# A fused two-layer forward pass on one Trainium2 core: the opening loads its norm weights with the transposed input, squares that input instead of `x`, and splits the third weight chunk in quarters

## The chip, the cores and the metric

The kernel runs on one core of a Trainium2 chip, as one program on five engines: TensorE (PE, with its weight loads shown as PEld), VectorE (DVE), ScalarE (ACT), GpSimd (POOL) and SyncE (SP), which here only starts DMA transfers. The metric is the device time of one execution in microseconds (us), lower is better. Everything is float32.

## The reference, cut to what matters

256 tokens of width 2048 pass through two layers. The part that the change touches is the first normalization and the first projection:

```python
def rms_norm(x, w):
    y = xf * lax.rsqrt(jnp.mean(xf * xf, axis=-1, keepdims=True) + EPS)
    return (y * w.astype(jnp.float32)).astype(x.dtype)
...
h = rms_norm(x, norm_mix_pre[l])
proj = jnp.einsum('bsd,dc->bsc', h, w_in[l])          # 2048 x 10240
qa, ka, va, qn, kn, vn, gates = jnp.split(proj, split_at, axis=-1)
qa = apply_rope(...); ka = apply_rope(...)            # first 2048 columns
...
x = x + rms_norm(y, norm_mix_post[l])                 # x itself is first needed here
```

After it come differential and neighbourhood attention, two gated projections, an output projection, a feed-forward part of width 8192, and a second layer with its own mixers. All of that is left as it is.

## The kernel before, in words

The work is a fixed sequence of 342 weight **chunks**. A chunk is four slices of 128 rows of a weight matrix, mostly 512 columns wide, so 1 MB. For each chunk, SP loads it into one of three `RAW` buffers. ACT copies it to `HI` (rounded to float32r, `high`, L506). DVE writes the remainder `LO = RAW - HI` (`low`, L922). PE then multiplies: for each 128-row slice and each of two token halves `t`, three products are accumulated in `acc`: input high by weight high, input high by weight low, input low by weight high. That makes 24 matmuls of 128x512 to a chunk. The input is split likewise in `ATH` and `ATL`.

The opening differs. `XT` holds the input transposed (16 slices of 128 features by 256 tokens). `x_high(k)` (ACT, L531) multiplies slice k by its norm weight and rounds it, `x_low(k)` (DVE, L926) makes the remainder. The factor 1/rms of a token is not applied there: it is a scale per row (`R0`) when a finished block of 512 columns is read out of `acc` (`evac`). It comes from the sum of squares of `x` (two ACT squares over `XS`, step `x sq`), a mean on DVE, and a power on POOL (`root`, named `r0`). Chunks 0 and 1 are loaded and split in quarters of 128x512 (`first`, L847 on ACT and L932 on DVE). Chunks alternate between column blocks 0 and 1: chunks 0, 2, 4, 6 make block 0, and 1, 3, 5, 7 block 1; chunks 2g and 2g+1 need slices 4g to 4g+3 of the input. `ahead` says that the splits of chunk n+2 stand at chunk n. A block of kind `rope` is read out on DVE: two multiplications by cosine and sine (L912) and two sums (L904) per token half. Then PE transposes the result, four 128x128 pieces each (`to_heads`, L1425).

The order on each engine is the order of the code, with semaphore waits in between. Before its first real work PE runs 20 small products on the constant tile `rst` (`warm`). SP's list of loads at the start is written out by hand in `sync`: whatever stands in it waits for all issues ahead of it. ACT starts the norm weights (`col`, all the per-feature vectors together, 69 KB) and the first four slices of `XT` from its own queue.

Of the kernel before, what the change touches and what calls it, by code (L numbers as in the profile page):

```python
# [7 lines left out]
F32 = mybir.dt.float32  # L8
# [21 lines left out]
C_PRE, C_MLP, C_N2, C_PE, C_CW, C_CB, C_LB, C_SUB, C_NW, C_IN = 0, 16, 32, 48, 64, 96, 104, 120, 122, 138  # L30
# [39 lines left out]
def program(nc, x, xt, w_in, w_a, w_b, w_out, w_up, w_down, w_in2, w_out2, w_pg, w_pe, p2,  # L70
            cols, lamv, rpb, rows, bif, cos_c, sin_c, nam_c, id_c, lvl_c, caus_c, out):
    with ExitStack() as ctx:
# [23 lines left out]
        ST = sb("st", [P, 96])  # L96
        MHALF = sb("mhalf", [P, 16])
# [82 lines left out]
        XT = m(32, 4096).rearrange("p (k s) -> p k s", k=16)  # L180
# [101 lines left out]
        for n, j, t in ((7, 0, 0), (7, 0, 1), (8, 1, 0), (9, 1, 1)):  # L282
# [54 lines left out]
        for g in range(1, 4):  # L337
            behind[2 * g - 2] = [("x", g, 0)]
# [12 lines left out]
        xt_ = xt.rearrange("p (k s) -> p k s", k=16)  # L351
# [3 lines left out]
        def sync(e):  # L355
# [11 lines left out]
            for n in range(2):  # L367
                for j in range(4):
                    load(RAW[n][:, 512 * j:512 * j + 512], w_in[j * P:(j + 1) * P, 512 * n:512 * n + 512], "first", n, j)
# [8 lines left out]
            raw(6)  # L378
            load(IDN[:, :], id_c[0], "id")
            load(LAMV, lamv.partition_broadcast(P), "lam")  # L380
            raw(7)
            load(NAM, nam_c, "nam")
            load(LVL[:, :, :, :], lvl_c, "lvl")
            load(CAU[:, :], caus_c, "cau")
            load(BIF[:, :], bif, "bif")
            for n in order[8:]:
                if n == 25:
# [32 lines left out]
        def gpsimd(e):  # L420
# [12 lines left out]
            e.memset(MHALF[:, :], -0.5).then_inc(s_pool.on("mhalf"))  # L433
            po.wait_ge(s_pool, LAST)
            e.memset(RST[:, :], 1.0).then_inc(s_pool.on("rst 1"))
            po.wait_ge(s_pool, LAST)
            e.memset(RST[:, 0:S:64], 0.0).then_inc(s_pool.on("rst"))
            for n in range(N_ALL):
                if n == 4:
# [49 lines left out]
        def scalar(e):  # L489
# [39 lines left out]
            def x_high(k):  # L529
                ac.wait_ge(loaded("col"), "col")  # L530
                e.activation(ATH[:, k, :], XT[:, k, :], ACT.Copy, scale=COL[:, C_PRE + k:C_PRE + k + 1]).then_inc(  # L531
# [19 lines left out]
            def da(u):  # L551
                if 0 <= u - 3:
                    v = u - 3
                    h, t = divmod(v, 2)
                    ac.wait_ge(s_pe, "da back", v)
# [1302 lines left out]
```

## Time and profile before

| | |
|---|---|
| median of 3 runs | 1990.64 us (1989.63 to 1991.04) |
| the profiled execution | 1989.69 us, of which its span is 1987.9 us |
| PE busy | 1968.0 us (99%), 9456 matmuls |
| DVE, ACT busy | 1210.1 us (61%), 987.4 us (50%) |
| DMA | 369.25 MB, mean 186 GB/s |

The time of a run has 1.8 us outside the span in the profiled execution. PE is the engine whose busy share fills the span. The profile's busy time of PE takes matmuls that overlap their neighbours at their whole duration, so the start times of successive matmuls tell more than the busy share. The granted TensorE clock is 0.998 of full over the span.

### The profile page before, as it was taken

How to read it: one execution, taken by the hardware profiler on the slowest of the kernel's cores; microseconds unless marked ns; L12 is line 12 of the kernel's file. 1: busy time of each engine (PE TensorE's matmuls, PEld its weight loads, DVE VectorE, ACT ScalarE, POOL GpSimd, SP SyncE). 2: the span in 40 equal slices, each digit the busy share in tenths (PEclk: the TensorE clock that was granted, in tenths of full speed). 3: DMA queues.
4: the chain of work that ended last, by engine and by line, in shares of the span. 5: the costliest groups of instructions: out<-in, count | busy, mean ns of one | idle time of the engine just before them, and what ended most of it. 6: DMA issues, size and time to landing. Idle time of an engine off the chain costs nothing.

```text
span 1987.9 us, 22811 instructions
## 1 busy us (share of the span) xinstructions
PE 1968.0 (99%) x9456; PEld 1651.6 (83%) x9456; DVE 1210.1 (61%) x1142; ACT 987.4 (50%) x953; POOL 39.8 (2%) x42
## 2 busy tenths in 40 slices
PE   9999999999999999999999999999999999999998
PEld 7888888888888888888888888888889888878886
DVE  5746446644656655445566666677567869676564
ACT  6345544445445444444455555565455545444454
POOL 0000000000000000000000000000000000230000
PEclk9999999999999999999999999999999999999999
DMA  8663555555657356655555555565556454445462
GB/s 319 207 201 129 170 191 183 178 178 190 221 181 254 119 178 189 192 184 182 185 190 192 192 196 197 197 214 189 170 154 203 164 172 158 153 165 206 169 212 106
DMA packets 186009, 369.25 MB, mean 186 GB/s; under 512 B 6829, under 2 KB 14257, under 8 KB 185265
## 3 DMA queue, kind: packets, MB, share of 16 engines
q1 hardware_dynamic: 184888, 366.27, 55.5%
q8 instruction: 74, 1.21, 0.2%
q10 hardware_dynamic: 1016, 1.52, 0.2%
q14 instruction: 31, 0.25, 0.0%
HBM read 365.66 MB, written 2.10 MB: 185 GB/s over the span
## 4 chain that ended last, share of the span: by engine, by line
PE 92%; DVE 3%; ACT 2%; issue 1%; DMA 1%; SPq 1%; ACTq 0%; POOLq 0%; POOL 0%; DVEq 0%
PE acc L1422 78%; PE mis L1422 12%; PE mis L1425 2%; ACT hi L506 1%; DVE lo L922 1%; DVE m L904 1%; DMA raw<-in_w_in 1%; SPq L359 0%; DMA m<-in_xt 0%; DVE m L908 0%; ACT m L495 0%; DVE m L912 0%; ACT sm L496 0%; ACT L495 0%; DVE sm L912 0%
## 5 line engine op out<-in xcount | busy, mean ns | idle before, releaser
L1422 PE MATMUL acc<-hi,at 128*128 128x512 f32 (+1 forms) x4384 | 1368.9, 390 | 1.8 <-DVE lo L932 1.3
L922 DVE TENSOR_TENSOR lo<-raw,hi 128x2048 fp32r<-128x2048 f32 (+1 forms) x334 | 756.9, 2269 | 569.4 <-ACT hi L506 567.3
L1422 PEld LDWEIGHTS acc<-hi,at 128*128 128x128 f32 x4384 | 821.1, 188 | 166.5 <-DVE at L926 1.7
L506 ACT ACTIVATE hi<-raw 128x2048 fp32r<-128x2048 f32 (+1 forms) x334 | 630.8, 1891 | 447.8 <-PE acc L1422 382.2
L1422 PE MATMUL acc<-lo,at 128*128 128x512 f32 (+1 forms) x2192 | 847.1, 386 | 0.0
L1422 PEld LDWEIGHTS acc<-lo,at 128*128 128x128 f32 x2192 | 412.5, 188 | 80.0
L1422 PE MATMUL mis<-at,hi 128*128 128x512 f32 x512 | 181.4, 398 | 0.0
L1422 PE MATMUL acc<-at,hi 128*128 128x512 f32 x448 | 158.5, 398 | 0.0
L1422 PE MATMUL mis<-at,lo 128*128 128x256 f32 x512 | 142.7, 281 | 0.0
L1422 PE MATMUL acc<-at,lo 128*128 128x256 f32 x448 | 124.5, 280 | 0.0
L1422 PEld LDWEIGHTS mis<-at,hi 128*128 128x128 f32 x512 | 96.2, 188 | 22.9
L495 ACT ACTIVATE m<-mis 128x256 f32<-128x256 f32 (+2 forms) x73 | 40.0, 548 | 145.7 <-PE mis L1425 86.8
L1422 PEld LDWEIGHTS acc<-at,hi 128*128 128x128 f32 x448 | 84.2, 188 | 20.1
L1422 PEld LDWEIGHTS mis<-at,lo 128*128 128x128 f32 x512 | 96.7, 189 | 0.7
L904 DVE TENSOR_TENSOR m<-m 128x256 f32<-128x256 f32 (+1 forms) x147 | 76.6, 521 | 22.2 <-ACT m L495 17.2
L495 ACT ACTIVATE m<-m 128x1024 f32<-128x1024 f32 (+4 forms) x51 | 53.2, 1042 | 71.0 <-DVE m L904 57.3
L1422 PEld LDWEIGHTS acc<-at,lo 128*128 128x128 f32 x448 | 84.6, 189 | 0.6
L495 ACT ACTIVATE m<-acc,st 128x512 f32<-128x512 f32 (+2 forms) x74 | 49.1, 663 | 65.4 <-PE acc L1422 64.6
L1422 PE MATMUL mis<-m 128*128 128x128 f32 (+3 forms) x384 | 73.9, 327 | 6.6 <-DVE m L912 6.1
L959 DVE TENSOR_TENSOR at<-m,at 128x1024 fp32r<-128x1024 f32 x64 | 78.0, 1218 | 4.1 <-ACT at L539 4.1
L539 ACT ACTIVATE at<-m 128x1024 fp32r<-128x1024 f32 x64 | 66.7, 1042 | 6.6 <-PE mis L1422 6.6
L1422 PEld LDWEIGHTS mis<-m 128*128 128x128 f32 x384 | 56.9, 191 | 14.6 <-DVE m L912 6.7
(126 smaller groups left out, 734.8 us busy)
## 6 DMA issues: line engine op xcount, KB each, us to landing
raw<-in_w_in SPq DMA_DIRECT2D x134, 1024.0 KB, 5.0
raw<-in_w_up SPq DMA_DIRECT2D x64, 1024.0 KB, 5.4
raw<-in_w_down SPq DMA_DIRECT2D x64, 1024.0 KB, 5.1
raw<-in_w_out SPq DMA_DIRECT2D x32, 1024.0 KB, 5.1
raw<-in_w_pg SPq DMA_DIRECT2D x16, 1024.0 KB, 5.1
raw<-in_w_in SPq DMA_DIRECT2D x12, 688.0 KB, 4.2
raw<-in_w_a SPq DMA_DIRECT2D x8, 1024.0 KB, 5.1
raw<-in_w_b SPq DMA_DIRECT2D x8, 1024.0 KB, 5.1
```

What stands on the lines that cost most here:

```text
L495: return e.activation(o, i, f, scale=scale, bias=bias)
L506: e.activation(hi_of(n), raw_of(n), ACT.Copy).then_inc(s_hi.on("hi", n))
L539: e.activation(ATH[:, 4 * (i % 4):4 * (i % 4) + 4, :], UT[:, 4 * (i % 16):4 * (i % 16) + 4, :], ACT.Copy).then_inc(s_ach.on("cut hi", i))
L904: return e.tensor_tensor(o, a, b, op)
L922: e.tensor_tensor(lo, raw, hi.bitcast(F32), ALU.subtract).then_inc(s_lo.on("lo", n))
L959: e.tensor_tensor(ATL[:, s4:s4 + 4, :], UT[:, k:k + 4, :], ATH[:, s4:s4 + 4, :].bitcast(F32), ALU.subtract).then_inc(s_dve.on("cut", i))
L1422: return e.matmul(o, a, b, start=start, stop=stop)
L1425: return e.transpose(o, a, IDN[:, :])
```

## The change

It has these parts.

1. The first norm's weights no longer come in `cols`. They stand as 16 columns ahead of the transposed input in HBM and land with its slice 0, in the 16 words ahead of `XT` (`PRE`). `cols` (now 122 columns) is loaded from SP ahead of chunk 11.
2. ACT's four slices of `XT` come as four transfers, not three. ACT splits a weight quarter ahead of its input slice, not behind it.
3. SP loads the second quarter of `XT` (slices 4 to 7) ahead of chunk 2, and chunk 2 in quarters. The input units of group g stand ahead of chunk 2g's splits, not behind.
4. `x` isn't loaded in the opening but at chunks 41 and 43. The squares are taken of `XT` (four ACT squares of 128x1024 into the room of `XS`), added and reduced over slices on DVE, and summed over partitions by PE with a column of ones (`x_sums`, behind chunk 5).
5. PE's products in chunk 0 go by operand: both token halves of high by high, then of input low, then of weight low, each with its own wait. There are 18 warming products, not 20, and POOL makes `rst` first.
6. The transposes of the first block's second token half stand inside chunk 8, between its token halves, not behind chunk 7.
7. Small loads are reordered: chunk 6 ahead of cosine, sine and identity; `nam`, `lvl`, `cau`, `bif` at chunk 11.

```diff
+        for n, j, t in ((7, 0, 0), (8, 0, 1), (8, 1, 0), (9, 1, 1)):
             beside(n, "heads", "rope", j, t)
+        amid = {(8, 1): ("rope", 0, 1)}
+        beside(5, "x_sums")
...
-            behind[2 * g - 2] = [("x", g, 0)]
+            before[2 * g - 2, 0] = [("x", g, 0)]
+        squares = {1: (0, 1), 3: (2,), 4: (3,)}
...
-            for n in range(2):
+            for n in range(3):
+                if n == 2:
+                    load(XT[:, 4:8, :], xt_[:, 4:8, :], "xt", 1)
                 for j in range(4):
+                    k, c = 4 * (n // 2) + j, 512 * (n % 2)
+                    load(RAW[n][:, 512 * j:512 * j + 512], w_in[k * P:(k + 1) * P, c:c + 512], "first", n, j)
-            raw(2)
-            for g in range(1, 4):
+            raw(3)
+            for g in range(2, 4):
                 load(XT[:, 4 * g:4 * g + 4, :], xt_[:, 4 * g:4 * g + 4, :], "xt", g)
                 raw(2 + g)
-            for t in range(2):
-                load(XS[:, t, :], xv[:, t, :], "x", t)
+            raw(6)
...
+                if n in (41, 43):
+                    t = (n - 41) // 2
+                    sp.wait_ge(s_dve, "r0")
+                    load(XS[:, t, :], xv[:, t, :], "x", t)
...
-            e.dma_start(COL[:, :], cols).then_inc(loaded("col").on("col"), 16)
-            for k, c in ((0, 1), (1, 1), (2, 2)):
-                e.dma_start(XT[:, k:k + c, :], xt_[:, k:k + c, :]).then_inc(loaded("xt", 0, k).on("xt", 0, k), 16)
+            e.dma_start(M[:, 32 * KB - 16:33 * KB], xt[:, 0:16 + KB]).then_inc(loaded("xt", 0, 0).on("xt", 0, 0), 16)
+            for k in range(1, 4):
+                e.dma_start(XT[:, k, :], xt_[:, k, :]).then_inc(loaded("xt", 0, k).on("xt", 0, k), 16)
...
             for j in range(4):
+                first(0, j)
+                ac.wait_ge(loaded("xt", 0, j), "xt", 0, j)
                 x_high(j)
-                first(0, j)
...
-                if n == 4:
-                    for t in range(2):
-                        ac.wait_ge(loaded("x", t), "x", t)
-                        act(m(48, 2048), XS[:, t, :], ACT.Square, accum=ST[:, t:t + 1]).then_inc(s_act.on("x sq", t))
+                for g in squares.get(n, ()):
+                    if g:
+                        ac.wait_ge(loaded("xt", g), "xt", g)
+                    act(XSQ[:, 4 * g:4 * g + 4, :], XT[:, 4 * g:4 * g + 4, :], ACT.Square).then_inc(s_act.on("x sq", g))
...
+                for g in squares.get(n, ()):
+                    if g:
+                        dv.wait_ge(s_act, "x sq", g)
+                        tt(XSQ[:, 0:4, :], XSQ[:, 0:4, :], XSQ[:, 4 * g:4 * g + 4, :], ALU.add).then_inc(s_dve.on())
+                    if g == 3:
+                        then()
+                        e.tensor_reduce(XSQ[:, 4, :], XSQ[:, 0:4, :].rearrange("p k s -> p s k"), AXX, ALU.add).then_inc(
+                            s_dve.on("x sums"))
+                if n == 5:
+                    dv.wait_ge(s_pe, "x sums")
+                    mean(2, mis[:, place.get(("x sums",), 0), 0:2], 2, D, "r0")
...
+            def x_sums():
+                z = take(("x sums",), s_dve, "r0")
+                pe.wait_ge(s_dve, "x sums")
+                pe.wait_ge(s_pool, "one")
+                for t in range(2):
+                    r = mm(mis[:, z, t:t + 1], XSQ[:, 4, t * P:(t + 1) * P], ONE[:, 0:1], True, True)
+                r.then_inc(s_pe.on("x sums"))
...
-            warm(20, 0)
+            warm(18, 0)
```

PE's instructions in chunk 0 before, behind the warming products (`hi0`, `lo0` are the split weights of chunk 0, `at` the split input, `s_weights_lo` and `s_dve_side` are raised by DVE):

```order
L1422 MATMUL acc<-rst 128x256 x19
L1422 MATMUL acc<-hi0,at 128x512 [waits s_weights_lo,s_dve_side]
L1422 MATMUL acc<-lo0,at 128x512
L1422 MATMUL acc<-hi0,at 128x512 x2
L1422 MATMUL acc<-lo0,at 128x512
```

The same place now; `s_weights_hi` and `s_act_high` are raised by ACT:

```order
L1452 MATMUL acc<-rst 128x256 x17
L1452 MATMUL acc<-hi0,at 128x512 [waits s_weights_hi,s_act_high]
L1452 MATMUL acc<-hi0,at 128x512
L1452 MATMUL acc<-hi0,at 128x512 [waits s_dve_side]
L1452 MATMUL acc<-hi0,at 128x512
L1452 MATMUL acc<-lo0,at 128x512 [waits s_weights_lo]
L1452 MATMUL acc<-lo0,at 128x512
```

The first two products of a slice now wait for ACT alone; DVE's two results are waited for later.

ACT's order behind the first two chunks' quarters, before (`at` is `x_high`, `m,st<-xs` the squares of `x`):

```order
L506 ACTIVATE hi2<-raw2 128x2048 [waits s_raw2]
L531 ACTIVATE at<-m,col 128x256 [waits s_load_xt_1]
L531 ACTIVATE at<-m,col 128x256 x3
L506 ACTIVATE hi0<-raw0 128x2048 [waits s_raw0,s_products]
L506 ACTIVATE hi1<-raw1 128x2048 [waits s_raw1,s_products]
L531 ACTIVATE at<-m,col 128x256 [waits s_load_xt_2]
```

And now:

```order
L544 ACTIVATE at<-m 128x256 [waits s_load_xt_1]
L544 ACTIVATE at<-m 128x256 x3
L861 ACTIVATE hi2<-raw2 128x512 [waits s_load_first_2_0]
L861 ACTIVATE hi2<-raw2 128x512 [waits s_load_first_2_1]
L861 ACTIVATE hi2<-raw2 128x512 [waits s_load_first_2_2]
L861 ACTIVATE hi2<-raw2 128x512 [waits s_load_first_2_3]
L520 ACTIVATE hi0<-raw0 128x2048 [waits s_raw0,s_products]
L509 ACTIVATE xs<-m 128x1024 [waits s_act_side] x2
L544 ACTIVATE at<-m 128x256 [waits s_load_xt_2]
```

Chunk 2 comes in quarters behind the input slices, and two squares stand between chunk 3's copy and the next input slices.

SP's order of loads behind chunk 2, before:

```order
L364 DMA raw0<-in_w_in 128x4x512 [waits s_weights_lo]
L359 DMA m<-in_xt 128x1024
L364 DMA raw1<-in_w_in 128x4x512 [waits s_weights_lo]
L359 DMA m<-in_xt 128x1024
L364 DMA raw2<-in_w_in 128x4x512 [waits s_weights_lo]
L359 DMA xs<-in_x 128x2048 x2
L359 DMA m<-in_cos 128x2x64
L359 DMA m<-in_sin 128x2x64
L364 DMA raw0<-in_w_in 128x4x512 [waits s_weights_lo]
```

And now:

```order
L369 DMA raw0<-in_w_in 128x4x512 [waits s_weights_lo]
L364 DMA m<-in_xt 128x1024
L369 DMA raw1<-in_w_in 128x4x512 [waits s_weights_lo]
L364 DMA m<-in_xt 128x1024
L369 DMA raw2<-in_w_in 128x4x512 [waits s_weights_lo]
L369 DMA raw0<-in_w_in 128x4x512 [waits s_weights_lo]
L364 DMA m<-in_cos 128x2x64
```

Chunk 6, the last of these, is issued directly behind chunk 5; the two loads of `x` are gone from here.

## Rows read from the trace of the kernel before

**Rows 1.** Who waited for whom, PE alone: total us, times, longest

```profile
PE mis L1422 <- DVE m L912: 6.1, 2, 4.2
PE acc L1422 <- POOL rst L437: 1.4, 1, 1.4
PE acc L1422 <- DVE lo L932: 1.3, 1, 1.3
PE mis L1425 <- DVE m L904: 1.0, 1, 1.0
PE acc L1422 <- DVE at L926: 0.5, 1, 0.5
```

**Rows 2.** Timeline of PE: start us, us, line, tiles, count, idle before

```profile
1.44 4.45 PE L1422 MATMUL acc<-rst 128*128 128x256 bf16 x20 [1.44 <-POOL rst L437]
7.16 0.77 PE L1422 MATMUL acc<-hi,at 128*128 128x512 f32 x1 [1.27 <-DVE lo L932]
...
10.25 0.40 PE L1422 MATMUL acc<-lo,at 128*128 128x512 f32 x1
...
19.37 0.39 PE L1422 MATMUL acc<-hi,at 128*128 128x512 f32 x1
20.25 0.47 PE L1422 MATMUL acc<-hi,at 128*128 128x512 f32 x1 [0.49 <-DVE at L926]
...
53.05 0.60 PE L1425 MATMUL mis<-idn,m 128*128 128x128 f32 x4
54.61 0.66 PE L1425 MATMUL mis<-idn,m 128*128 128x128 f32 x4 [0.96 <-DVE m L904]
55.02 0.47 PE L1422 MATMUL acc<-hi,at 128*128 128x512 f32 x1
```

**Rows 3.** Timeline of ACT in the opening

```profile
3.92 0.20 ACT L495 ACTIVATE mhalf<-mhalf 128x1 f32<-128x1 f32 x1
5.26 0.51 ACT L531 ACTIVATE at<-m,col 128x256 fp32r<-128x256 f32 x1 [1.13 <-DMA m<-in_xt]
5.67 0.61 ACT L847 ACTIVATE hi<-raw 128x512 fp32r<-128x512 f32 x1
7.75 0.51 ACT L531 ACTIVATE at<-m,col 128x256 fp32r<-128x256 f32 x1 [1.47 <-DMA m<-in_xt]
...
8.98 0.51 ACT L531 ACTIVATE at<-m,col 128x256 fp32r<-128x256 f32 x1 [0.20 <-DMA m<-in_xt]
...
18.35 1.92 ACT L506 ACTIVATE hi<-raw 128x2048 fp32r<-128x2048 f32 x1 [0.56 <-DMA raw<-in_w_in]
...
35.72 1.92 ACT L506 ACTIVATE hi<-raw 128x2048 fp32r<-128x2048 f32 x1 [6.46 <-DMA raw<-in_w_in]
```

**Rows 4.** Timeline of DVE in the opening

```profile
11.05 3.09 DVE L932 TENSOR_TENSOR lo<-raw,hi 128x512 fp32r<-128x512 f32 x5
...
20.30 2.29 DVE L922 TENSOR_TENSOR lo<-raw,hi 128x2048 fp32r<-128x2048 f32 x1 [0.20 <-ACT hi L506]
```

**Rows 5.** DMA of the first 10 us: total, and an issue with KB, median us to landing

```profile
DMA packets 1672, 2.61 MB, mean 261 GB/s; under 512 B 178, under 2 KB 562, under 8 KB 1672
...
col<-in_cols ACTq DMA_DIRECT2D x1, 69.0 KB, 3.6
```

**Rows 6.** Stretches of 1 us: PE, PEld, DVE, ACT, POOL busy, clock, DMA share, GB/s

```profile
5.00:6.00 1.00, 0.89 (x5) 0.30 (x2) 0.20 (x1) 0.74 (x2) 0.00 (x0) 1.00 0.78 219
9.00:10.00 1.00, 1.00 (x4) 0.71 (x3) 0.98 (x2) 1.00 (x3) 0.00 (x0) 1.00 1.05 406
```

**Rows 7.** Groups by form on ACT and DVE: total us, mean ns

```profile
L495 ACT ACTIVATE m<-m 128x1024 f32<-128x1024 f32 x39 | 41.3, 1060 | 48.6 <-DVE m L904 37.9 <-DVE m L912 10.4
L904 DVE TENSOR_TENSOR m<-mis,m 128x1024 f32<-128x1024 f32 x8 | 9.8, 1224 | 18.3 <-ACT m L495 18.3
L996 DVE TENSOR_REDUCE st<-mis 128x2 f32<-128x512 f32 x8 | 5.5, 691 | 2.5 <-PE mis L1422 1.8
```

**Rows 8.** Timeline of PE at the gates' small float32 products

```profile
1540.09 1.05 PE L1422 MATMUL mis<-idn,sm 4*128 4x4 f32 x8
```

More of the change, by code:

```diff
@@ L96, in program @@
         ST = sb("st", [P, 96])
+        ONE = sb("one", [P, 1])
         MHALF = sb("mhalf", [P, 16])
@@ L437, in gpsimd @@
             e.memset(RST[:, 0:S:64], 0.0).then_inc(s_pool.on("rst"))
+            po.wait_ge(s_pool, LAST)
+            e.memset(MHALF[:, :], -0.5).then_inc(s_pool.on("mhalf"))
+            po.wait_ge(s_pool, LAST)
+            e.memset(ONE[:, :], 1.0).then_inc(s_pool.on("one"))
             for n in range(N_ALL):
-                if n == 4:
+                if n == 5:
                     root(2, 2, "r0")
@@ L529, in x_high @@
             def x_high(k):
-                ac.wait_ge(loaded("col"), "col")
-                e.activation(ATH[:, k, :], XT[:, k, :], ACT.Copy, scale=COL[:, C_PRE + k:C_PRE + k + 1]).then_inc(
+                e.activation(ATH[:, k, :], XT[:, k, :], ACT.Copy, scale=PRE[:, k:k + 1]).then_inc(
                     s_ach.on("ath", "x", k))
@@ L555, in da @@
                     ac.wait_ge(s_pe, "da back", v)
+                    ac.wait_ge(loaded("col"), "col")
                     for c in range(2):
@@ L868, in scalar @@
                 for c in ahead.get(n, ()):
-                    if c not in spare:
+                    if c == 2:
+                        for j in range(4):
+                            first(c, j)
+                    elif c not in spare:
                         high(c)
@@ L1042, in prep @@
                     a0, a1 = COL[:, C_LB:C_LB + 8], COL[:, C_LB + 8:C_LB + 16]
+                    dv.wait_ge(loaded("col"), "col")
                     tt(LB, a0, a1, ALU.max).then_inc(s_dve.on())
@@ L1389, in vector @@
                 for c in ahead.get(n, ()):
-                    if c not in spare:
+                    if c == 2:
+                        for j in range(4):
+                            first(c, j)
+                    elif c not in spare:
                         low(c)
@@ L1491, in products @@
                 for j in range(4):
-                    if n == 1 and t == 0:
+                    if n in (1, 2) and t == 0:
                         pe.wait_ge(s_lo, *(("lo first", n, j) if j < 3 else ("lo", n)))
@@ L1744, in turnover @@
                     products(c, 1)
[L1746 removed]
+            do = dict(x_sums=x_sums, da=da, na=na, rb=rb, ut=ut, gate=gate, turn_v=turn_v, hg=hg, ml=ml)
             turn[0] = 0
             held.clear()
[L1749 removed]
+            warm(18, 0)
             first()
@@ L1763, in tensor @@
                         unit(*u)
+                    if (n, t) in amid:
+                        kind, j, tt_ = amid[n, t]
+                        to_heads(R[tt_], number[kind, j], tt_, kind, j, tt_)
                     if blocks[chunks[n][2]][0] == "upw":
@@ L1771, in tensor @@
                 for name, *i in side.get(n, ()):
-                    if name == "heads":
+                    if name == "heads" and tuple(i) not in amid.values():
                         kind, j, t = i
@@ L1827, in lay_out @@
     rpb = np.asarray(i["na_rpb"])[0][:, dr, dc].reshape(8, 2, P, S).transpose(0, 2, 1, 3).reshape(8, P, 2 * S)
-    cols = [col(i[n]) for n in ("norm_mix_pre", "norm_mlp_pre", "norm_w_2", "pe_norm_w_2")]
+    cols = [col(i[n]) for n in ("norm_mlp_pre", "norm_w_2", "pe_norm_w_2")]
     cols += [col(i[n]) for n in ("conv_w_2", "conv_b_2", "hg_lb_2", "subln_w", "ml_norm_w_2", "hg_norm_w_2")]
@@ L1835, in lay_out @@
     c = constants()
-    return [("x", two("x")), ("xt", turned(two("x"))), ("w_in", two("w_in")), ("w_a", two("w_branch_a")), ("w_b", two("w_branch_b")),
+    return [("x", two("x")), ("xt", np.concatenate([col(i["norm_mix_pre"]), turned(two("x"))], 1)), ("w_in", two("w_in")), ("w_a", two("w_branch_a")), ("w_b", two("w_branch_b")),
             ("w_out", two("w_out")), ("w_up", two("w_up")), ("w_down", two("w_down")), ("w_in2", two("w_in_2")),
```

49 lines of the change are left out of this document (23 added, 26 removed).

## The prediction

> **What bounds the kernel now.** I read the list of waits first. PE is named as waiting in few places: 1.4 us for the constant tile, 1.3 us for the first remainder, 0.5 us for an input slice, 1.0 us for a rope result, and 6.1 us in the second layer that the change doesn't touch [rows 1]. Everywhere else PE has its next operands when it wants them, so the time is PE's own work plus these gaps. Only the opening, to about 55 us, can give anything.
>
> The timeline of PE then sizes the opening [rows 2]. Four things are lost there. (a) The first real product starts at 7.16, although the warming products end at 5.89. (b) Over chunks 2 to 7 the pace is (53.05 - 20.25) / 6 = 5.47 us a chunk, 0.228 us a matmul. Chunks 0 and 1 (48 matmuls, 10.9 us at that pace) take from 7.16 to 20.25, 13.1 us: 2.2 us too much. The first seven real matmuls fill 7.16 to 10.25, 0.44 us each, and the warming ones run at 0.222 us for 256 columns, so until 10.25 the array goes at the lower of its two levels (1.2 against 2.4 GHz), which 1.5 us of the 2.2 are; the rest is the wait ahead of chunk 2 (19.6 to 20.25). (c) Between 53.05 and 55.02 stand two sets of transposes. A set costs 55.02 - 54.61 = 0.41 us, so 1.97 - 0.82 = 1.15 us there is waiting for the second token half of the first rope block. (d) 1.44 us pass ahead of everything.
>
> ACT's timeline says what is late [rows 3]: it waits for input slices at 5.26, 7.75 and 8.98, and for chunk 3's weights until 18.35. Chunk 6's weights come only at 35.72, after 6.46 us of idling, and this is what makes DVE late for the rope block. The DMA engines are full: a share of 1.05 and 406 GB/s already at 9 us [rows 6].
>
> **The change part by part.**
>
> *Start of PE.* ACT is free at 3.92 + 0.20 = 4.12. The input slice with the norm weights is now first in ACT's queue, issued at 0.75. The transfer that stood there, `col`, took 3.6 us, so it landed at 4.35 [rows 5]; the slice behind it came at 5.26 [rows 3]. The new one (139 KB) lies between these bounds, 4.35 and 5.26. I take 4.7, nearer to the first, because it is in the same place. With the weight quarter split in the 0.6 us before, ACT's slice is ready about 5.3. PE's 18 warming products from about 1.3 last 18 x 0.222 = 4.0 us, to 5.3. The first real product starts about 5.4, 1.8 us sooner, since it waits for ACT alone and DVE's two steps (from ACT's 5.67 to 7.16 before) lie beside the first products.
>
> *Chunks 0 and 1.* PE's earlier start doesn't count whole, as the data of chunk 0 still trickle in. In the old run the last two input slices were there at 8.98 and ACT then made them one after the other, with a weight quarter between; now a slice waits for its own transfer and the weight quarter is split while it comes. I put the last input slice on ACT at about 9.0 (before, 8.98 and a step of slice and quarter, about 0.9, later: 5.67 - 5.26 is 0.41 of it), the last remainder of chunk 0 on DVE from 10.0 to 10.65 (before 11.05 to 11.7) [rows 4]. PE ends chunk 0 at about 11.2. Chunk 1's remainders follow at 0.6 us each, so they are ready ahead of PE, and chunk 1 ends at 11.4 + 5.47 = 16.9, where before chunk 2 started at 20.25. This takes the array to be at the upper level from about 8 us at the latest: the 1.27 us gap between warming and work is nearly closed (5.3 to 5.4), and before, the level rose at 10.25, 3.1 us into the real products that followed that gap. If the rise stays at 10.1, 11 matmuls are done by then at 0.43 us, and 37 remain at 0.228: 18.5.
>
> The Trainium skill ("TensorE: Matmul & The Clock Gate", What's actually happening) says that the number of matmuls at the lower level varies from run to run of one kernel. By it the 18.5 and the 16.9 would be two outcomes of the same program; one trace can't show that.
>
> *Chunk 2* needs input slices 4 to 7, now ahead of it in the queue, and its own quarters. The bytes up to and with chunk 2 are those of before, 4.2 MB. 2.61 MB have moved by 10 us [rows 5], and the rest at 0.4 MB/us ends at about 14.0; with a delay from last byte to use of about 1.4 us, which the same count gives for chunk 3 (5.3 MB, by 16.8, used at 18.35), the quarters land up to about 15.4. ACT and DVE then finish the first remainder at 16.0 and the last at 17.7, 0.6 us apart, while PE uses one each 0.68 us. PE starts chunk 2 at 16.9 without a wait. The 0.65 us ahead of chunk 2 are gone.
>
> *Chunk 3 becomes the bound.* Its weights are in the same place in the queue, and landed at 18.3 before, with the DMA engines full. ACT then takes 1.92 us and DVE is done at 20.30 + 2.29 = 22.6 [rows 3, 4]. PE is there at 16.9 + 5.47 = 22.4 and starts at 22.65. Before, it started at 20.25 + 5.47 = 25.72. The gain is 3.05 us here, and no earlier start of chunk 0 can add to it unless these weights land sooner. In the 18.5 case PE comes at 24.0 and the gain is 1.75.
>
> *Squares.* ACT's four squares of 128x1024 cost 1.06 us each [rows 7]; two stand ahead of the input slices of chunk 4, from 20.3 to 22.4. The four slices follow to 24.1, the weights (6.9 MB into the queue, so landed by about 22.1) to 26.0, DVE's remainder to 28.2. PE wants it at 22.65 + 5.47 = 28.1: a wait of 0.1. DVE's first sum (1.22 us, [rows 7]) runs from 22.6 to 23.8 and isn't in the way. For chunk 5 DVE is done about 31.5 against 33.7, for chunk 6 at about 36.8 against 39.2: covered by some 2 us each. If the cover were gone, the squares' 4.2 us on ACT and about 4.9 us on DVE would be on the path.
>
> *x_sums.* DVE's last sum and the reduction follow chunk 6's remainder: 36.8 + 1.2 + 1.2 = 39.2. PE asks for it at 39.1, so it is just hidden or 0.1 late. For the reduction the trace has no strided form; the contiguous 128x512 takes 0.69 us [rows 7], which gives 1.2 for 1024 elements as the lower end, and four times that, 4.9, is my upper end. I take 1.2, nearest to the row. PE's own part is two float32 products, each split in two by the hardware as the gates' four are in eight: half of 1.05 us [rows 8], 0.5 us. Queued behind them is chunk 6, so this is on the path.
>
> *x late, and the rope wait.* Without 2 MB of `x` (5.2 us at 400 GB/s) ahead of it, chunk 6 lands about 29 instead of 35.7. Chunk 7 and 8 are split by 44, and DVE is free for the first rope block when chunk 6 ends on PE (45.0). Each token half takes 2.45 us, so they are ready at 47 and 49.5, and PE comes at 50.6 and later. The 1.15 us of (c) are saved; the transposes moved inside chunk 8 have cover beyond that (2.7 us). The loads of `x` at chunks 41 and 43 cost two issues of 0.5 us on SP and 2.6 us of DMA each, with the engines about half idle there; chunk weights are asked for more than a chunk ahead. I cost this at nothing; uncovered it would be at most 5.2 us.
>
> *The remaining loads* and the moved vectors (`cols`) go to where DMA has room, and PE's instruction count grows by the two products alone.
>
> **Sum.** 3.05 - 0.1 - 0.5 + 1.15 = 3.6 us, less 0.1 for a late reduction: 3.5 us. Against the profiled execution's 1989.69 that is 1986.2. Its time lies 0.95 us below the median of the runs shown, and against the median, 1990.64, the same 3.5 us give 1987.1. A measurement of this kernel can't tell less than about 0.2% (4.0 us) from no change, and the bound is at 1986.66: the forecast is a gain, most likely just inside it.
>
> **The rivals.**
>
> *The array's level rises as late as before* (18.5 for chunk 1's end). For it: 4.45 us of warming didn't raise it in the old run. Against it: the gap after the warming is what goes. The gain is 1.75 - 0.5 + 1.15 = 2.4 us, 1988.2. Chance 0.18.
>
> *Quarter loads bring less.* In the stretch from 5 to 6 us, when only small transfers were in flight, the rate was 219 GB/s, at 9 us 406 [rows 6]. If chunk 2's 1.05 MB and the slices went at about 310 GB/s, chunk 3's weights would land 1.0 us later and all behind them too: gain 2.5 us, 1988.1. For it speaks only the early dip, which a start of transfers explains as well. Chance 0.10. The Trainium skill ("DMA: Bandwidth & Descriptors", Measured) advises loads of 1 MB and more, by a fixed cost of about 2 us each; its rule would speak for this rival, or, with the quarters one after another, 6 us on chunk 2. The 406 GB/s with quarters in flight disagree with the strong form.
>
> *Chunk 3 comes sooner.* If freeing the queue of `col` and asking for chunk 3 about 1 us earlier (DVE frees its buffer at 10.65, not 11.7) bring it in before 18.3, PE isn't held at 22.65 and the whole of 20.25 - 16.9 = 3.35 and up to 1 us more in chunk 0 counts: gain 4.2 to 5.0, about 1986.0. Chance 0.17.
>
> *The sums hold PE.* PE waits behind chunk 5 for a reduction that is slow over strides. At 4.9 us it is done at 42.9, PE loses 3.8 us, and the result is 1990.9, slower than before by 0.3 us. It decides from 4.7 us for the reduction; to be over 0.2% slower it needs 8.7 us. Chance 0.05, of it 0.02 beyond 0.2%.
>
> *The change does nothing*, as a gap given back further on, where PE runs ahead of weights: 1990.6. In the old run nothing waits on weights behind 55 us. Chance 0.03.
>
> **How the numbers follow.** The forecast has 0.47, with a range of its own from 1986.2 to 1987.9; about two fifths of it, 0.19, lies under 1986.66. With the 0.17 of the sooner chunk 3 and a little of the others for the spread of runs (1989.63 to 1991.04), faster by over 0.2% has 0.38, within 0.2% 0.59, slower 0.03. The range is 1985.4 to 1989.3: from nearly the best case to the late level and the slow quarters with the runs' spread, leaving out the sums that hold PE and the null case.
>
> **What would show it.** The first real product at 5.2 to 5.6. Start times 0.228 us apart from about 8. Chunk 2's first product at 16.9 without a wait on an input slice. A wait for the remainder of chunk 3 at about 22.6: if it isn't there, the weights came sooner. Two pairs of small products behind chunk 5 costing 0.5 us. No wait of over 0.2 us at the rope transposes, and chunk 8's first product near 51.2 against 55.02. It would be wrong if PE is seen waiting for sums behind chunk 5, for weights around 41 to 45, or if the level rises at 10 again.

## The result, and the profile after

The changed kernel takes 1986.04 us (median of 13 runs, 1984.69 to 1987.02), the kernel before on the same chip 1989.82 us (13 runs, 1987.95 to 1991.04). The ratio is 0.9983, with a 95% interval of 0.9976 to 0.999. Between the medians stand 3.8 us, between the profiled executions 3.6 us (1986.09 against 1989.69, spans 1984.3 and 1987.9). The forecast was 3.5 us, and the 3.8 us between the medians (0.19%) are clear of the spread of the runs, since the interval leaves out 1.

PE's list of waits after the change (total us, times, longest), to be held against [rows 1]:

```profile
PE mis L1452 <- DVE m L929: 6.1, 2, 4.2
PE acc L1452 <- POOL rst L447: 1.3, 1, 1.3
PE mis L1452 <- DVE m L921: 0.5, 1, 0.5
PE mis L1452 <- DVE xs L1426: 0.3, 1, 0.3
```

The waits for the first remainder (1.3), for the input slice ahead of chunk 2 (0.5) and for the rope block (1.0) are gone. One is new, 0.3 us for the reduction of the squares. The second layer's 6.1 us stand as they did.

PE's timeline (start us, us, line, tiles, count, idle before), against [rows 2]:

```profile
1.27 4.02 PE L1452 MATMUL acc<-rst 128*128 128x256 bf16 x18 [1.27 <-POOL rst L447]
5.10 1.91 PE L1452 MATMUL acc<-hi,at 128*128 128x512 f32 x4
6.85 0.63 PE L1452 MATMUL acc<-lo,at 128*128 128x512 f32 x2
...
11.40 0.39 PE L1452 MATMUL acc<-hi,at 128*128 128x512 f32 x1
...
16.62 0.62 PE L1452 MATMUL acc<-hi,at 128*128 128x512 f32 x2
...
22.06 0.62 PE L1452 MATMUL acc<-hi,at 128*128 128x512 f32 x2
...
38.38 0.39 PE L1452 MATMUL acc<-hi,at 128*128 128x512 f32 x1
39.06 0.61 PE L1452 MATMUL mis<-one,xs 128*128 128x1 f32 x4 [0.30 <-DVE xs L1426]
39.53 0.48 PE L1452 MATMUL acc<-hi,at 128*128 128x512 f32 x1
...
50.52 0.60 PE L1455 MATMUL mis<-idn,m 128*128 128x128 f32 x4
...
53.73 0.60 PE L1455 MATMUL mis<-idn,m 128*128 128x128 f32 x4
...
57.28 0.48 PE L1452 MATMUL acc<-hi,at 128*128 128x512 f32 x1
```

The first real product starts at 5.10. The first four are 0.44 us apart on average (6.85 - 5.10 over 4; one by one they start at 5.10, 5.70, 6.12 and 6.55), all later ones about 0.227: the upper level is there from 6.85 at the latest. Chunk 1 begins at 11.40. Chunk 2 begins with the second product of the row at 16.62, so at 16.85, where it was 20.25. Chunk 3 begins in the same way at 22.29 and waits for nothing. Behind chunk 5 (its last product at 38.38, done at 38.61) PE stands until the two small products, and chunk 6 starts at 39.53. Neither set of transposes at 50.52 and 53.73 waits. Chunk 9 starts at 57.28. This last moment serves as the measure in all that follows, since chunk 8 is cut by transposes in one version and not in the other. In the kernel before it is this row:

```profile
60.93 0.48 PE L1422 MATMUL acc<-hi,at 128*128 128x512 f32 x1
```

Chunk 3 of the kernel before begins with the second product of this row, so at 25.81:

```profile
25.58 0.62 PE L1422 MATMUL acc<-hi,at 128*128 128x512 f32 x2
```

The 3.65 us between the two starts of chunk 9 are the whole difference: from there to the end of the span it takes 1927.0 us in both.

ACT and DVE, where they answer to [rows 3, 4]. ACT:

```profile
4.04 0.61 ACT L861 ACTIVATE hi<-raw 128x512 fp32r<-128x512 f32 x1
4.56 0.49 ACT L544 ACTIVATE at<-m 128x256 fp32r<-128x256 f32 x1
...
17.34 1.92 ACT L520 ACTIVATE hi<-raw 128x2048 fp32r<-128x2048 f32 x1 [1.68 <-DMA raw<-in_w_in]
```

DVE:

```profile
19.29 2.29 DVE L939 TENSOR_TENSOR lo<-raw,hi 128x2048 fp32r<-128x2048 f32 x1 [2.66 <-ACT hi L520]
...
35.76 1.22 DVE L921 TENSOR_TENSOR xs<-xs 128x1024 f32<-128x1024 f32 x1
37.02 1.99 DVE L1426 TENSOR_REDUCE xs<-xs 128x256 f32<-128x1024 f32 x1
```

No input slice is waited for at the start any more. Chunk 3's weights are on ACT at 17.34, 1.0 us sooner than before, and their remainder is done at 19.29 + 2.29 = 21.58, 0.7 us ahead of PE. The reduction over strides takes 1.99 us.

The stretches of the first microseconds (busy shares, clock, DMA share, GB/s), against [rows 6]:

```profile
6.00:7.00 1.00, 1.00 (x4) 0.76 (x4) 0.59 (x3) 0.86 (x3) 0.00 (x0) 1.00 1.07 397
9.00:10.00 1.00, 1.00 (x6) 0.84 (x5) 1.00 (x3) 0.95 (x3) 0.00 (x0) 1.00 1.10 418
```

With quarters of 256 KB, the small slices and one load of 512 KB (input slices 4 to 7, issued at 4.69) in flight, and none of 1 MB before 9.95, the DMA engines move 397 to 418 GB/s.

### The profile page after: what moved, and what is told of

Read it like the earlier page. It is cut to its first block, busy times and chain, and to the rows that moved or that the text cites. A ratio compares the mean times of both kernels' runs of the same rounds, so it can differ in the third digit from the quotient of the medians.

```text
span 1984.3 us, 22830 instructions
## 1 busy us (share of the span) xinstructions
PE 1967.0 (99%) x9458; PEld 1651.5 (83%) x9458; DVE 1215.8 (61%) x1149; ACT 988.0 (50%) x956; POOL 41.8 (2%) x43
## 4 chain that ended last, share of the span: by engine, by line
PE 93%; DVE 3%; ACT 2%; issue 2%; DMA 1%; SPq 0%; POOLq 0%; POOL 0%; DVEq 0%; ACTq 0%
PE acc L1452 79%; PE mis L1452 12%; PE mis L1455 2%; ACT hi L520 1%; DVE m L921 1%; DVE lo L939 1%; DMA raw<-in_w_in 1%; DMA m<-in_xt 0%; DVE m L925 0%; ACT m L509 0%; ACT sm L510 0%; SPq L364 0%; ACT L509 0%; DVE xs L921 0%; DVE lo L949 0%
```

## The experiments

The theory: the gain is that chunk 2's data come sooner (input slices ahead, quarters), and the first slice with its norm weights, which starts PE sooner; what is left is the rope block. The rivals: it is the array's earlier level alone, PE's order of products, or `x` out of the way of chunk 6. The first run is on the last of these. All kernels compute the whole reference. For each the text gives the start of chunk 9, since whole times also carry up to 2.5 us that arise in the second layer, as the last section shows.

### x_early: `x` back ahead of chunk 6, the squares still of the transposed input

```diff
-        XSQ = XS.rearrange("p t d -> p (t d)").rearrange("p (k s) -> p k s", k=16)
+        XSQ = m(48, 4096).rearrange("p (k s) -> p k s", k=16)
...
+            for t in range(2):
+                load(XS[:, t, :], xv[:, t, :], "x", t)
             raw(6)
...
-                if n in (41, 43):
-                    t = (n - 41) // 2
-                    sp.wait_ge(s_dve, "r0")
-                    load(XS[:, t, :], xv[:, t, :], "x", t)
```

> The changed kernel, but x is loaded ahead of chunk 6 as in the old order (the squares use other room, the rest is kept). Theory (late x is what brings chunk 6 in time): ACT's copy of chunk 6 starts at about 35 instead of 31.05, its remainder is done about 39.3, the sum and reduction behind it on DVE at about 42.5, and PE waits there some 3.9 us instead of 0.3; chunk 9's first product at about 60.8 instead of 57.28, so the time is about 3.5 us longer, that of the kernel before. Rival (x in the opening is hidden as in the old run, and only the rope transposes wait): chunk 9 at about 58.3, 1 us longer. Rival (x costs nothing): 57.3.

Measured: 1990.78 us (10 runs), 1.0009 of before (1.0 to 1.0019); chunk 9 at 63.23 (forecast 60.8, with a longer wait of 3.9 us and no fall of the level). ACT got chunk 6 at 34.41, and the last sum, behind it on DVE, came late for PE:

```profile
41.77 0.99 PE L1450 MATMUL mis<-one,m 128*128 128x1 f32 x4 [2.78 <-DVE m L1424]
42.62 0.77 PE L1450 MATMUL acc<-hi,at 128*128 128x512 f32 x1
43.19 0.63 PE L1450 MATMUL acc<-lo,at 128*128 128x512 f32 x1
43.62 1.05 PE L1450 MATMUL acc<-hi,at 128*128 128x512 f32 x2
```

The stretches show what the wait cost beside itself:

```profile
42.00:43.00 1.00, 1.00 (x5) 1.00 (x6) 1.00 (x1) 1.00 (x1) 0.00 (x0) 0.50 0.93 358
...
48.00:49.00 1.00, 1.00 (x5) 0.79 (x4) 0.77 (x2) 0.00 (x0) 0.00 (x0) 0.67 1.09 359
49.00:50.00 1.00, 1.00 (x6) 0.83 (x5) 0.97 (x2) 0.00 (x0) 0.00 (x0) 1.00 1.08 367
```

The granted clock is 0.50 (1.2 GHz) from about 42 to 48.6, products 0.43 us apart. Chunk 6 starts at 42.62 and chunk 7 at 51.02, 8.4 us apart where it is 5.55 in the changed kernel: some 3 us lost in addition to the 2.78. The whole loss is 63.23 - 57.28 = 5.95 us. So with the sums placed at chunk 5, `x` must not stand ahead of chunk 6: the two halves of part 4 hang together.

### chunk2_whole: chunk 2 as one load ahead of the second input quarter

```diff
-            for n in range(3):
-                if n == 2:
-                    load(XT[:, 4:8, :], xt_[:, 4:8, :], "xt", 1)
+            for n in range(2):
...
-            raw(3)
+            raw(2)
+            load(XT[:, 4:8, :], xt_[:, 4:8, :], "xt", 1)
+            raw(3)
```

(Not shown: on ACT and DVE chunk 2 is split in one piece, and input slices 4 to 7 stand behind it again.)

> The changed kernel, but chunk 2 is one load, ahead of input slices 4 to 7, and split before them, as before. Theory (the slices behind chunk 2 on ACT and DVE held PE at 20.25): slices' remainders are done at about 19.2, PE waits there about 2.3 us, chunk 2 starts at 19.2 instead of 16.85, and chunk 9 at about 59.3 (the 0.3 us wait for the sums is absorbed), 2 us longer. Rival (the bytes are the same, so chunk 2 is ready at 16.85 anyway): chunk 9 at 57.3, the same time.

Measured: 1988.12 us (10 runs), 0.9994 (0.9984 to 1.0003); chunk 9 at 61.08 in the profiled execution, so there nearly the whole gain is gone (forecast 59.3). PE at chunk 2:

```profile
19.45 0.47 PE L1449 MATMUL acc<-hi,at 128*128 128x512 f32 x1 [2.17 <-DVE at L943]
```

Chunk 2 starts 2.60 us later than at 16.85, by the wait for the input slices that was forecast. Less the 0.56 us that the sums no longer wait, that makes 59.3 at chunk 9. The other 1.8 us are the level again, 0.50 from 21 to 24:

```profile
21.00:22.00 1.00, 1.00 (x4) 0.78 (x3) 1.00 (x2) 1.00 (x3) 0.00 (x0) 0.50 0.98 379
```

The profiled execution, 1989.77 us, is the second slowest of the ten. Their median is 1.65 us shorter and 2.1 us longer than the changed kernel's 1986.04, about what the wait alone costs. So the 2.0 us of the wait are the safe reading; whether the other runs had the lowered level isn't recorded. This run undoes the order of the loads and the quarters together: PE waits for the input slices, and what the quarters bring by themselves is not measured.

### old_pe_order: chunk 0's products in the old order

```diff
-                    a, c = ([z[:, j, t * P:t * P + P] for t in range(2)] for z in (ATH, ATL))
-                    pe.wait_ge(s_ach, "ath", "x", j)
-                    pe.wait_ge(s_hi, "hi first", 0, j)
-                    for t in range(2):
-                        mm(acc[:, t, :], a[t], hv[:, j, :], j == 0, False)
                     pe.wait_ge(s_dve, "atl", "x", j)
-                    for t in range(2):
-                        mm(acc[:, t, :], c[t], hv[:, j, :], False, False)
                     pe.wait_ge(s_lo, *(("lo first", 0, j) if j < 3 else ("lo", 0)))
                     for t in range(2):
-                        r = mm(acc[:, t, :], a[t], lv[:, j, :], False, False)
...
+                        mm(acc[:, t, :], a, hv[:, j, :], j == 0, False)
+                        mm(acc[:, t, :], a, lv[:, j, :], False, False)
+                        r = mm(acc[:, t, :], c, hv[:, j, :], False, False)
```

> The changed kernel, but PE's products in chunk 0 in the old order, waiting for both remainders of a slice. The first real product comes at about 6.25 instead of 5.10, after a gap of 1.0 us behind the warming products. Theory (a gap of that size keeps the array at the lower level until about 10, as in the old run): chunk 0 ends at about 13.6, chunk 9 starts at about 59.1. Rival (the level rises at about 6.8 whatever the gap): chunk 0 ends at about 11.9, chunk 9 starts at about 57.5.

Measured: one run of 1984.47 us; chunk 9 at 57.35. The first real product is 1.4 us later and the second comes 0.30 behind it:

```profile
6.47 0.47 PE L1452 MATMUL acc<-hi,at 128*128 128x512 f32 x1 [1.18 <-DVE lo L949]
6.77 0.40 PE L1452 MATMUL acc<-lo,at 128*128 128x512 f32 x1
```

The array is at its upper level at once, so the theory that a gap of this size keeps it down (59.1) is refuted, and chunk 2 starts at 17.44, 0.6 us later than in the changed kernel. The sums cost 0.36 us here and not 0.92, which takes up 0.56 of it. Between these two traces the order by operand was worth 0.07 us; against the second trace of the changed kernel (after_again, 56.72) it is 0.63. So its worth isn't settled, and where nothing waits at the sums the 0.6 us might count: no run shows that.

### before_warm26: the kernel before, with 26 warming products

```diff
-            warm(20, 0)
+            warm(26, 0)
```

> The kernel before with 26 warming products instead of 20, so that they end as the first real product starts (7.2). Theory for the clock (the gap held it low): matmuls start 0.228 us apart from soon after 7.2, where the old run had 0.44 until 10.25, and chunk 1 ends at about 17.8 instead of 19.6. Theory for the time (chunk 2 is held by input slices 4 to 7 until 20.1, whatever comes ahead): chunk 2 starts at 20.2 all the same, and chunk 9 at 60.9, so no gain. Rival: chunk 2 moves with chunk 1, and chunk 9 starts 1.5 us sooner, at 59.4.

Measured: one run of 1990.74 us; chunk 9 at 61.13. PE in the opening:

```profile
7.05 0.47 PE L1422 MATMUL acc<-hi,at 128*128 128x512 f32 x1 [0.79 <-DVE lo L932]
7.36 0.40 PE L1422 MATMUL acc<-lo,at 128*128 128x512 f32 x1
...
18.65 0.39 PE L1422 MATMUL acc<-hi,at 128*128 128x512 f32 x1
20.07 0.47 PE L1422 MATMUL acc<-hi,at 128*128 128x512 f32 x1 [1.03 <-DVE at L926]
```

The level is up from the first product, chunk 1 ends at 18.88, and all of it is given back ahead of chunk 2, which starts at 20.07 for want of its input slices. An early level alone is worth nothing in the old opening: chunk 2's data are the bound. This and chunk2_whole are the two halves of one argument.

### before_x_late: the kernel before, with part 4 alone

```diff
+        beside(5, "x_sums")
+        squares = {1: (0, 1), 3: (2,), 4: (3,)}
...
-            for t in range(2):
-                load(XS[:, t, :], xv[:, t, :], "x", t)
```

(The squares, their sums on DVE and PE and the loads of `x` at chunks 41 and 43 are those of the changed kernel.)

> The kernel before with only the fourth part of the change: squares of the transposed input, x loaded at chunks 41 and 43. Theory (x ahead of chunk 6 is what made the rope block late): chunk 2 starts at 20.25 as before, chunk 6's weights are copied by ACT near 32 instead of 35.7, the rope wait of 1.15 us goes and the two sum products cost 0.5: chunk 9 at about 60.3 instead of 60.93. Rival (the wait stays, as DVE has 5.6 us more to do): about 61.4.

Measured: one run of 1988.84 us; chunk 9 at 60.34, forecast 60.3. ACT has chunk 6 at 31.57 where it was 35.72, and the transposes stand together without a wait:

```profile
53.65 1.03 PE L1442 MATMUL mis<-idn,m 128*128 128x128 f32 x8
```

The eight pieces take 0.79 us (53.65 to 54.44), where the kernel before spent 1.97. So about 1.2 us are won at the rope block, 0.36 paid for the small products and 0.16 lost by chunk 2 (20.41), about 0.6 in all. As a total that is no more than two traces of one program differ by (after_again); that the wait of 0.96 us is gone is plain.

The start of this trace says something else, on the array's level. The opening and its 20 warming products are those of the kernel before, and the gap is longer (1.41 us), yet the upper level is there at once:

```profile
7.16 0.47 PE L1439 MATMUL acc<-hi,at 128*128 128x512 f32 x1 [1.41 <-DVE lo L940]
7.47 0.39 PE L1439 MATMUL acc<-lo,at 128*128 128x512 f32 x1
```

Chunk 2 starts at 20.41 all the same, which says once more that this level is worth nothing there.

### x_old: the changed kernel with all of part 4 undone

```diff
-        beside(5, "x_sums")
...
+            for t in range(2):
+                load(XS[:, t, :], xv[:, t, :], "x", t)
             raw(6)
...
+                if n == 4:
+                    for t in range(2):
+                        ac.wait_ge(loaded("x", t), "x", t)
+                        act(m(48, 2048), XS[:, t, :], ACT.Square, accum=ST[:, t:t + 1]).then_inc(s_act.on("x sq", t))
```

> The changed kernel with its fourth part wholly undone: x loaded ahead of chunk 6 and squared from there by ACT as before, no sums on DVE and PE; all other parts stay. Theory A (x late is needed once PE runs 3.4 us sooner): chunk 6 is split at about 38.7 and the squares hold ACT until 40.4, so chunks 7 and 8 and the rope block come late, chunk 9 starts at 59 or later. Theory B (the other parts are enough, since the second transposes stand inside chunk 8 and the 0.9 us at the sums falls away): PE waits about 0.6 us ahead of chunk 7 and chunk 9 starts at about 57.0, no later than the changed kernel's 57.28.

Measured: 1985.78 us (10 runs), 0.998 (0.997 to 0.9989); chunk 9 at 57.21. ACT still waits for chunk 6:

```profile
34.77 1.92 ACT L517 ACTIVATE hi<-raw 128x2048 fp32r<-128x2048 f32 x1 [4.25 <-DMA raw<-in_w_in]
```

No wait of PE is named in the opening, and the sums' 0.9 us are saved. But DVE is done with chunk 6 only at 39.01 and with chunk 7 at about 44.8, and PE's first two products of each straddle these moments:

```profile
38.68 0.89 PE L1441 MATMUL acc<-hi,at 128*128 128x512 f32 x2
44.41 0.95 PE L1441 MATMUL acc<-hi,at 128*128 128x512 f32 x2
```

The three chunks from 5 to 7 take 16.98 us (33.47 to 50.45) where three at full pace take 16.3: some 0.66 us are lost. The rope block's transposes, one set of them inside chunk 8, find DVE done. So what part 4 saves at chunks 6 and 7 it pays for at the sums, and in the changed opening it is worth nothing that these runs can show, 57.21 against 57.28.

### x_after6: as x_old, with `x` loaded behind chunk 6

```diff
             raw(6)
+            for t in range(2):
+                load(XS[:, t, :], xv[:, t, :], "x", t)
```

(The rest as in x_old.)

> As x_old, but x is loaded directly behind chunk 6 instead of ahead of it. If only the place of x in SP's list matters, and not what is squared, chunk 6 is in time (ACT copy near 31), ACT squares x at 35 to 39, and nothing waits: chunk 9 on PE at about 56.4, 0.9 us sooner than the changed kernel, the 0.9 us being the two sum products and the wait for them. If the squares of x on ACT still hold chunk 7 back, PE waits ahead of it, and chunk 9 starts at 57.5 or later.

Measured: 1984.80 us (10 runs), 0.9976 (0.9967 to 0.9986); chunk 9 at 56.44, forecast 56.4. It has the lowest median of the versions that were run ten times. ACT has chunk 6 at 29.65, squares `x` from 31.46 on, and PE has no small products and no wait for them:

```profile
29.65 1.91 ACT L517 ACTIVATE hi<-raw 128x2048 fp32r<-128x2048 f32 x1
31.46 1.90 ACT L507 ACTIVATE m<-xs 128x2048 f32<-128x2048 f32 x1
```

What part 4 wanted, chunk 6 in time, one place in the order of loads gives without the small products: chunks 5 to 7 take 5.44 us each here. Against the changed kernel it is 0.84 us by the start of chunk 9 in its first trace and 0.28 in its second; the two intervals against before overlap. So that it is faster than the changed kernel is likely, not shown.

### sum_tree: two contiguous sums in place of the strided reduction

```diff
-                        then()
-                        e.tensor_reduce(XSQ[:, 4, :], XSQ[:, 0:4, :].rearrange("p k s -> p s k"), AXX, ALU.add).then_inc(
-                            s_dve.on("x sums"))
+                        tt(XSQ[:, 0:2, :], XSQ[:, 0:2, :], XSQ[:, 2:4, :], ALU.add).then_inc(s_dve.on())
+                        tt(XSQ[:, 4, :], XSQ[:, 0, :], XSQ[:, 1, :], ALU.add).then_inc(s_dve.on("x sums"))
```

> The changed kernel, but the reduction over strides on DVE (1.99 us) is replaced by two more sums, of 512 and 256 columns (about 0.7 and 0.4 us). Theory (PE's 0.30 us wait behind chunk 5 is for this reduction): the wait goes, and chunk 9 starts on PE at about 57.0 instead of 57.28. Rival (something else holds PE there): 57.3.

Measured: one run of 1985.22 us; chunk 9 at 56.48. DVE's last three sums, and PE:

```profile
35.58 2.41 DVE L921 TENSOR_TENSOR xs<-xs 128x1024 f32<-128x1024 f32 x3
```

```profile
38.33 0.50 PE L1451 MATMUL mis<-one,xs 128*128 128x1 f32 x4
38.69 0.49 PE L1451 MATMUL acc<-hi,at 128*128 128x512 f32 x1
```

The three sums take 2.41 us, where a sum and the reduction took 3.25 (35.76 to 39.01), and PE doesn't wait: its products cost 0.36 us (38.69 - 38.33) of the 0.92, and the other 0.56 are gone. Of the 0.8 us at chunk 9, 0.27 are not the edit's: the level rose sooner here, and chunk 1 begins at 11.13 and not 11.40.

### col_first: the vectors `col` again first in ACT's queue

```diff
-                    load(COL[:, :], cols, "col")
...
+            e.dma_start(COL[:, :], cols).then_inc(loaded("col").on("col"), 16)
             e.dma_start(M[:, 32 * KB - 16:33 * KB], xt[:, 0:16 + KB]).then_inc(loaded("xt", 0, 0).on("xt", 0, 0), 16)
```

> The changed kernel, but the transfer of the per-feature vectors stands first in ACT's queue again, ahead of the input slice with the norm weights. Theory (the first transfer of that queue sets PE's start): slice 0 is scaled by ACT at about 5.25 instead of 4.56, the first real product comes at 5.75 instead of 5.10, and chunk 9 starts 0.3 to 0.6 us later than 57.28, at about 57.7, since the other slices come later too. Rival (the data of the later slices, or the wait for the sums behind chunk 5, bound PE anyway): chunk 9 at 57.3.

Measured: one run of 1987.83 us; chunk 9 at 58.38, 1.1 us later (forecast 57.7, 0.4 later). PE's start:

```profile
5.68 1.25 PE L1452 MATMUL acc<-hi,at 128*128 128x512 f32 x4 [0.39 <-ACT at L543]
...
7.89 1.25 PE L1452 MATMUL acc<-hi,at 128*128 128x512 f32 x4 [0.36 <-ACT at L543]
```

One more issue on ACT moves its table load from 2.64 to 3.13, and the next slices are on ACT 1.3 to 1.4 us later (7.33 for 6.05, 8.63 for 7.22). The delay isn't covered by anything: DVE's work is late with them, its reduction ending at 40.09 where it was 39.01, so that here the sums take nothing up as they did in old_pe_order.

### amid_undone: the second set of transposes back behind chunk 7

```diff
-        for n, j, t in ((7, 0, 0), (8, 0, 1), (8, 1, 0), (9, 1, 1)):
+        for n, j, t in ((7, 0, 0), (7, 0, 1), (8, 1, 0), (9, 1, 1)):
...
-        amid = {(8, 1): ("rope", 0, 1)}
+        amid = {}
```

> The changed kernel, but the transposes of the first block's second token half stand behind chunk 7 again. The second half is ready on DVE at about 49.2 and PE comes there at 50.9. Theory (with chunk 6 in time these transposes need no cover): chunk 9 at 57.3, no difference. Rival (the cover inside chunk 8 is what removed the 1.15 us): PE waits about 1 us there, chunk 9 at 58.3.

Measured: one run of 1984.24 us; chunk 9 at 57.15. All eight pieces stand at 50.46 with no wait, so with `x` late part 6 is worth nothing that can be seen.

### after_again: the changed kernel once more

> The changed kernel once more, unaltered, to see what differs between two executions of one program. If the moment at which the array goes from 1.2 to 2.4 GHz isn't fixed, the first real products at 0.43 us apart are more or fewer than four, chunk 0 ends at another time than 11.40 (by up to 0.9 us), and the stretch behind the waits near 1740 us differs by about 1.7 us. If it is fixed by what the engine did before, both are as in the first trace: 6.85 for the first matmul at the upper level, 6.1 us of waits there.

Measured: one run of 1985.41 us; chunk 9 at 56.72, 0.56 us sooner than in the first trace of the same program:

```profile
5.14 1.47 PE L1452 MATMUL acc<-hi,at 128*128 128x512 f32 x4
6.45 0.62 PE L1452 MATMUL acc<-lo,at 128*128 128x512 f32 x2
```

The level comes sooner: the first four products start at 5.14, 5.73, 5.98 and 6.21, so it is up from the second or third on, where the first trace has 5.10, 5.70, 6.12 and 6.55. Chunk 1 begins at 11.19 and not 11.40, and the sums have no named wait. Differences under about 0.6 us at chunk 9 between single traces are therefore not read as effects. x_old, old_pe_order and amid_undone are within it, and so are the totals of before_x_late (0.59) and x_after6 (0.28 against this trace).

## Why the prediction was right, and where it was not

By its own steps, with gains against the kernel before:

| step | forecast | measured |
|---|---|---|
| first real product | 5.4 | 5.10 |
| upper level from | 8 at the latest | 6.85 at the latest |
| chunk 1 starts | 11.4 | 11.40 |
| chunk 2 starts | 16.9, no wait | 16.85, no wait |
| chunk 3 starts, gain there | 22.65, 3.05 | 22.29, 25.81 - 22.29 = 3.52 |
| squares' cost | 0.1 | 0: chunks 3 to 5 take 5.44 us each in both kernels |
| sums: products and wait | 0.5 + 0.1 | 39.53 - 38.61 = 0.92, and less than 0.1 in chunk 6 behind them |
| rope block | 1.15 | 1.12: the gain is 53.05 - 50.52 = 2.53 ahead of it and 3.65 behind |
| sum | 3.5 | 3.65 at chunk 9 |

*Start and level.* Right in the times. PE starts 2.06 us sooner, and of this the larger part is the order of the products: with the old order it is 1.37 us later (old_pe_order, 6.47), with the slice second in its queue 0.58 (col_first, 5.68). The reason given for the level, that the gap after the warming products held it down in [rows 2], is not borne out: before_x_late has the same opening with a gap of 1.41 us, old_pe_order one of 1.18 and before_warm26 one of 0.79, and all three are at the upper level at once. That the changed kernel's level came before 8 was thus not due to the closed gap as far as these traces tell; what sets the moment stays open. The Trainium skill ("TensorE: Matmul & The Clock Gate", What's actually happening) lets the moment of the rise vary between runs of one kernel; the traces agree, with the third product 0.42 us behind the second in one trace of the changed kernel and 0.25 in the other.

*Chunk 0.* The number is right, the way to it is not. The forecast has data trickling in until DVE's last remainder at 10.65 and PE done at 11.2, and then goes on from 11.4 without a reason. That remainder was done at 9.93 (9.24 + 0.69), and PE waited for none after 5.10: it took its own 24 products, four of them at the lower level, until 11.40. That the 11.4 fits to the hundredth is luck.

*Chunk 2.* Right, and shown from both sides: chunk2_whole puts back the wait (2.17 us), and before_warm26 shows that without this part an earlier PE wins nothing. It is shown for the order and the quarters together.

*Chunk 3 as the bound.* This step failed, in the sense of its rival "chunk 3 comes sooner". The weights were asked for at 9.95, 1.8 us earlier, because DVE freed the buffer earlier, and were there at 17.34, not 18.3. PE found them ready, and the gain was the 3.4 us of chunk 2's start (20.25 - 16.85), as that rival had it, with 0.1 more because chunk 2 no longer begins behind a wait. The further 0 to 1 us that it added for chunk 0 didn't come, since the 16.9 at chunk 2 already held it.

*Sums.* The term was mis-sized. The reduction took 1.99 us where 1.2 was chosen at the lower end of 1.2 to 4.9, so PE waited; the products themselves took 0.36 us (sum_tree). The errors, 0.47 more at chunk 3 and 0.1 at the squares against 0.4 less at the sums, nearly cancel: the total was closer than its terms, and that is luck.

*Late `x` and the rope wait.* In size right (1.12; in before_x_late 1.2, of which 0.6 are left at chunk 9). As an account of what is needed it wasn't: in the changed opening either a late `x` or the transposes amid chunk 8 is enough, and undoing one of them changes nothing that these runs can show (x_old, amid_undone); both undone together wasn't run. The forecast named both without asking if one made the other idle.

*Quarter loads.* The rival that they bring less is false here: 397 to 418 GB/s, as at 9 us in [rows 6]. The Trainium skill ("DMA: Bandwidth & Descriptors", Measured) asks for 1 MB and more in a transfer, by figures for transfers issued from GpSimd; with quarters queued one behind the other by SP the trace disagrees.

*Sums that hold PE* was a true danger that the changed kernel nearly misses: in x_early the same products waited 2.78 us and the whole gain went. It was priced at the wait alone; the lowered clock doubled it. In the changed kernel the reduction ends at 39.01 and PE asks at 38.61, and a second trace of it has no named wait: the order is late by a few tenths at most.

## What to carry to other kernels

Undo the parts of a change one at a time from the changed kernel as well as adding them to the old one. Here the loads of chunk 2 (input slices ahead of it, quarters) and the first place in ACT's queue carry the gain: undoing the first costs a wait of 2.2 us (2.1 us by the medians), undoing the second 1.1 us at chunk 9, in one trace each. The order of products, the moved transposes and the squares' new source show none beyond the 0.6 us by which two traces of one program differ, and what the last was for, a moved line of the load order gives as well (x_after6). An engine that is made earlier wins only up to the next transfer that bounds it, so look for that one first. And price a wait of 2 us or more on PE at up to twice its length: those of 2.78 and 2.17 us in the opening cost 5.6 and 4.0 where the lower level followed.

## What the runs showed that was not expected

**A PE wait of some 2 us or more may be followed by a stretch at the lower level, or may not.** In the second layer stand two such waits, 1.9 us and then 2.6 or 4.2 us, and the granted clock behind the second is 0.50 in most of the profiled executions. In the changed kernel:

```profile
1740.40 1.89 PE L1452 MATMUL mis<-m 128*128 128x257 f32 x4 [4.24 <-DVE m L929]
```

```profile
1741.00:1742.00 1.00, 1.00 (x5) 0.82 (x3) 0.41 (x1) 0.97 (x4) 0.00 (x0) 0.50 0.00 0
```

In amid_undone, at the same place:

```profile
1742.00:1743.00 1.00, 1.00 (x6) 0.82 (x5) 1.00 (x1) 1.00 (x3) 0.00 (x0) 1.00 0.00 0
```

From chunk 9 to the end of the span the 13 profiled executions fall in three groups: about 1925.3 us (x_early, old_pe_order, amid_undone; 1.00 behind the second wait), 1926.7 to 1927.0 (eight, about 3.5 us at 0.50) and 1927.6 to 1927.8 (col_first, before_warm26; 6 to 6.5 us at 0.50). The two traces of the changed kernel show that the program alone doesn't decide what happens there: in the first no drop follows the first of the two waits and the second lasts 4.2 us, in the second a drop does follow (0.50 from 1730 to 1732), and the second wait is 2.6 us, the difference being absorbed.

Over the 13 traces this makes a pattern. A drop follows the first wait, always 1.9 us long, in six; the second wait is then 2.5 to 2.6 us, and a second drop follows in three of them (after_again, before_x_late, x_after6) and not in the other three, which are the fastest group. In the seven without a drop behind the first wait the second is 4.2 us, and a drop always follows. What decides the first drop, and the second behind the shorter wait, stays open. Its 1.7 us are half of the gain studied here, which is why the starts of chunk 9 were compared.

**The first rise isn't seen in the granted clock of the stretches.** In the changed kernel it reads 1.00 from 5 to 6 us, while products start at 5.10, 5.70 and 6.12; only the start times show the level there.
